# Four weight blocks of the first unit: GpSimd makes the last two high parts of each

## The reference, cut to what matters

```
u    = rms_norm(x, norm_gain)
proj = jnp.einsum('btd,dc->btc', u, w_in).astype(f32)
```

## Time and profile before

| | |
|---|---|
| median of 3 runs | 2012.45 us |
| profiled execution | 2012.38 us |
| its span, first to last instruction | 2010.6 us |
| TensorE busy | 1960.3 us (98%), 12974 matmuls |
| VectorE busy | 1667.5 us (83%) |
| ScalarE busy | 876.1 us (44%) |
| GpSimd busy | 309.4 us (15%), 288 instructions |
| mean granted TensorE clock | 0.99 |

### The profile page before, as it was taken

The page is one execution under the profiler, slowest core; times in us unless marked ns, Lnnn a source line. Parts: engine busy times, 40 slices in busy tenths (PEclk is TensorE's granted clock), DMA queues, the critical chain, the costliest instruction groups (busy, mean ns, idle before and its releaser), DMA issues.

```text
span 2010.6 us, 36659 instructions
## 1 busy us (share of the span) xinstructions
PE 1960.3 (98%) x12974; PEld 1095.1 (54%) x12974; DVE 1667.5 (83%) x4034; ACT 876.1 (44%) x2246; POOL 309.4 (15%) x288
## 2 busy tenths in 40 slices
PE   6999999999999999999999999999999999999998
PEld 4555555555555555444465555555555555554453
DVE  7888888888888888664478888888888888898757
ACT  7844444444444446231265444444444444452100
POOL 3011111111111112120011111111111111111100
PEclk9999999999999999999999999999999999999989
DMA  9222222222222224885542232222222222458552
GB/s 338 54 41 61 51 50 50 50 62 58 50 50 50 50 62 133 192 264 155 177 142 61 57 65 50 50 50 50 54 59 54 60 50 50 107 142 198 140 136 95
DMA packets 303428, 184.17 MB, mean 92 GB/s; under 512 B 267847, under 2 KB 277000, under 8 KB 303180
## 3 DMA queue, kind: packets, MB, share of 16 engines
q1 hardware_dynamic: 287348, 151.41, 30.5%
q0 software_dynamic: 7424, 29.43, 4.1%
q10 hardware_dynamic: 8568, 2.18, 0.5%
HBM read 85.29 MB, written 41.06 MB: 63 GB/s over the span
## 4 chain that ended last, share of the span: by engine, by line
PE 85%; DVE 10%; ACT 2%; issue 2%; DMA 1%; SPq 0%; DVEq 0%; ACTq 0%
PE J L593 53%; PE J L1338 13%; PE W L1031 2%; PE W L1020 2%; PE W L1107 2%; PE W L1137 1%; PE J L1071 1%; PE W L1125 1%; PE W L1096 1%; PE T L1116 1%; ACT W L577 1%; DMA ST<-ST 1%; PE W L1038 1%; PE T L1081 1%; PE W L1109 1%
## 5 line engine op out<-in xcount | busy, mean ns | idle before, releaser
L593 PE MATMUL J<-W,uT_mix 128*128 128x512 f16 (+2 forms) x3072 | 609.1, 355 | 5.1 <-DVE W L584 4.3
L593 PE MATMUL J<-W,x_mix 128*128 128x512 f16 (+2 forms) x3072 | 604.4, 353 | 3.6 <-issue 2.2
L593 PEld LDWEIGHTS J<-W,uT_mix 128*128 128x128 f16 x3072 | 296.8, 99 | 275.6 <-issue 11.3
L593 PEld LDWEIGHTS J<-W,x_mix 128*128 128x128 f16 x3072 | 295.6, 98 | 270.9 <-issue 7.0
L1454 ACT ACTIVATE PB<-J,out_scale 128x512 f32<-128x512 f32 (+2 forms) x224 | 133.1, 594 | 286.6 <-PE J L593 278.4
L1338 PE MATMUL J<-W,EM_qkR_mix 128*128 128x512 f16 x480 | 115.3, 379 | 0.0
L2414 POOL TENSOR_TENSOR ST<-HH,ge 128x512 f32<-128x512 f32 x32 | 41.4, 1294 | 408.9 <-DVE HH L1884 408.9
L2423 POOL TENSOR_TENSOR ST<-ST,ge 128x512 f32<-128x512 f32 x32 | 67.9, 2121 | 216.0 <-DVE ST L1929 216.0
L1418 ACT ACTIVATE sc_xr<-sc_xr,small 128x128 f32<-128x128 f32 x256 | 98.5, 386 | 0.0
L1338 PE MATMUL J<-W,x_mix 128*128 128x512 f16 x400 | 98.0, 384 | 0.0
L1424 ACT ACTIVATE ST<-ST,small 128x1024 f16<-128x1024 f32 x32 | 36.7, 1148 | 140.2 <-DVE small L1945 140.2
(11 more groups left out here) (470 smaller groups left out, 3479.1 us busy)
## 6 DMA issues: line engine op xcount, KB each, us to landing
W<-in_w_in POOLq DMA_DIRECT2D x8, 2048.0 KB, 11.1
mix_d<-ST SPq DMA_DIRECT2D x32, 512.0 KB, 2.6
sc_xr<-in_x_prompt SPq DMA_DIRECT2D x20, 512.0 KB, 4.1
sc_xr<-x SPq DMA_DIRECT2D x20, 512.0 KB, 3.8
ST<-in_w_in POOLq DMA_DIRECT2D x4, 2048.0 KB, 11.9
W<-in_w_out SPq DMA_DIRECT2D x4, 2048.0 KB, 7.9
PB<-in_x_prompt SPq DMA_DIRECT2D x6, 512.0 KB, 3.8
x<-PB SPq DMA_DIRECT2D x6, 512.0 KB, 3.5
```

The costliest lines, as they stand in the source:

```text
L593: mm = nc.tensor.matmul(out, stationary(k, a), moving[:, k, b, :], start=(k == 0 and n == 0), stop=(k == KT - 1 and n == 2))
```

## The change

In layer 0 only, for blocks j = 4 to 7, ScalarE makes slices 0 to 5 of the high part (`HI_ACT = 6`), and a new function, `block_hi_end`, makes slices 6 and 7 on GpSimd with `tensor_scalar`. Each of GpSimd's slices waits for the block's scale, for the low part of the same slice of the block before, and for the count of `C["hi"]` up to it, so that the count stays in order. ScalarE's `block_hi` of blocks 5 to 7 gets a wait for all the high parts of the block before. On GpSimd the eight new multiplications stand after `first_rope` and the last load, ahead of `r_gate`.

```diff
+        HI_ACT = 6
 ...
         def block_hi(act, layer, j, ks=range(KT)):
 ...
+            if layer == 0 and j > 4:
+                act.wait_ge(C["hi"], KT * j)
 ...
+        def block_hi_end(pool, layer, j):
+            b = SAMPLE_ORDER[j]
+            pool.wait_ge(C["scale_ready"], NBLK * layer + j + 1)
+            for k in range(HI_ACT, KT):
+                pool.wait_ge(C["lo"], KT * (NBLK * layer + j - 1) + k + 1)
+                pool.wait_ge(C["hi"], KT * (NBLK * layer + j) + k)
+                nc.gpsimd.tensor_scalar(pair[b][:, k, 0, :], raw(layer, b)[:, k, :], gs[:, j, k:k + 1], None, ALU.mult
+                                        ).then_inc(C["hi"], 1)
 ...
-                block_hi(act, layer, 4)
+                block_hi(act, layer, 4, range(0, HI_ACT))
 ...
-                block_hi(act, layer, 5)
+                block_hi(act, layer, 5, range(0, HI_ACT))
 ...
-                block_hi(act, layer, 6, range(5, KT))
+                block_hi(act, layer, 6, range(5, HI_ACT))
 ...
-                block_hi(act, layer, 7)
+                block_hi(act, layer, 7, range(0, HI_ACT))
 ...
                 load_raw(pool, layer, "mvo")
+            else:
+                for j in range(4, NBLK):
+                    block_hi_end(pool, layer, j)
             c_pool.begin(pool, N0)
             r_gate(N0)
             m_gate(N0)
```

## The result

Five runs of the changed kernel took 2022.91 to 2029.55 us, median 2026.21; the kernel before, run beside it, 2008.77 to 2014.11. The ratio is 1.0064, 95% interval 1.0049 to 1.0079: slower by 12.9 us (9.9 to 15.9). The direction was forecast; 5.8 us and a range up to 2021.5 were not enough. The profiled execution took 2022.91, span 2021.1, mean granted clock 0.988.

What follows compares the result with a forecast made beforehand. TensorE was taken as the bound, with 85% of the chain. Block 4 at 0, blocks 5 to 7 at 3 x 2.04, less 0.4 and 0.25, plus 0.3, gave 5.8 us: 2012.38 to 2018.2, range 2013.5 to 2021.5.

Steps and rivals of the forecast that it cites:

- What is removed: Eight ScalarE multiplications, 5.0 us of ScalarE's time, none on the chain, so priced at 0.
- In series with VectorE: Blocks 5 to 7: GpSimd's multiplications and VectorE's low parts exclude each other, delaying each block's last low part 2.04 us.
- Rival 1: GpSimd gets its turn between two low parts without holding VectorE up; time 2012.0, not slower; chance 0.17.
- The forecast of 0 for block 4: Block 4: TensorE's slack of 2.7 us and VectorE's 2.50 idle hide the 2.04 us delay, costing 0.
- The price p: Time of one GpSimd multiplication of the new kind, taken as 0.85 us, with ends 0.61 and 1.27.
- d: Delay of a block's last low part, 2p + 0.34, where p is one GpSimd multiplication: 2.04 us, 1.56 to 2.88.
- The smaller terms: Block 7: 0.4 won at L2072 beside `r_gate`, 0.25 of TensorE's slack, 0.3 lost to `r_gate`.
- Rival 2: The clock falls as well, TensorE pausing twice in each of three products; one fall 2.9 us, 2021.1; chance 0.09.
- My row against it: Evidence against a clock fall: from 68 to 70 us TensorE was busy 0.88 of 2.00, the clock stayed at 1.00.
- Rival 3: First `tensor_scalar` on GpSimd pays for set-up, block 4's last low part passing its slack by 2 us; 2020.2; chance 0.04.

Runs made afterwards that it cites:

- the zero fill: Changed kernel with GpSimd only filling slices 6 and 7 of the high part with zero, reading nothing; ratio 1.0002 against the kernel before.
- the load alone: Kernel before, ScalarE making all slices, plus GpSimd repeating the eight multiplications into scratch that nobody reads; ratio 1.0007.
- the run of block 5 alone: Changed kernel with GpSimd making slices 6 and 7 of block 5 only; ratio 1.0026 against the kernel before.
- the run with one slice: Changed kernel with HI_ACT 7 instead of 6, so GpSimd makes slice 7 alone in blocks 4 to 7; ratio 1.0028 against the kernel before.
- two tensors: Changed kernel with GpSimd's multiplication as a two-tensor one, the scale column repeated 512 times; one run, 2023.21 us.
- with gaps: Changed kernel with a short VectorE reduction ahead of the low parts of slices 3, 4 and 5 of blocks 5 to 7; one run, 2021.12 us.
- second set: The changed kernel timed and profiled once more with no edit; ratio 1.0058 against the kernel before.
- its own count: Changed kernel with GpSimd's slices counting on their own semaphore, not waiting for ScalarE's slices 0 to 5; ratio 1.0015 against the kernel before.
- the run with both repairs: Changed kernel with GpSimd's slices on their own semaphore, not waiting for ScalarE's, and made as two-tensor multiplications; ratio 1.0004 against the kernel before.

## Why the prediction was wrong, step by step

- **What is removed: right.** ScalarE's 5.0 us were priced at 0; the zero fill, with the same relief, gives 29.8 and 1.0002.
- **In series with VectorE: right in blocks 5 to 7, wrong in block 4.** In blocks 5 to 7 VectorE idles before slices 6 and 7 with GpSimd as the releaser, slice 6 is the long one in block 5 (4.17 for 2.05), and the load alone costs 0.7. In blocks 6 and 7 it is hardly longer than slice 7 (2.18 and 2.19 for 2.05), since ScalarE's slice 5 came late. Rival 1 is out there. In block 4 it is what happened: GpSimd had its turns between low parts, and the last one came 0.7 us late, not 2.04. The forecast of 0 for block 4 held, but not for its reason.
- **The price p: the step that failed.** I took 0.85, from rows of another operation, and let it end at 1.27, the row of two full tensors. It measured 1.55 alone, and 1.44 from the end of VectorE's low parts. The formula was sound: 2 x 1.44 + 0.34 = 3.2 for d, measured 3.1 in block 5 and in the run of block 5 alone. With it the prediction's sum is 3 x 3.22 - 0.35 = 9.3 us, or 2021.7, just past the range's end; the clock makes the rest. What I had worked out from the row with the small operand, 1.03, is what the two-tensor form takes (1.02); I carried it to another instruction. The rule that "GPSIMD Engine Reference", section 4.1, of the Trainium skill states, one input at roughly line rate, gave 0.62; the measurement is 2.5 times that, and decides.
- **The smaller terms: right.** L2085 beside nothing takes 0.34 where it took 0.82, 0.48 won for 0.4 said; the last low part of block 7 takes 1.20 for 0.75, so `r_gate` cost 0.45 for 0.3 said.
- **Rival 2, the clock, came on top.** I gave it 0.09. Both profiles of the changed kernel have falls, in block 5 and in or behind block 7. In the first the price is 0.64 + 0.2 in block 5 (last slice, spread) and 0.64 + 0.9 in block 7 (last slice; the score products behind it end 1.9 us after it where they took 1.04 before), 2.4 in all. My row against it was one pause of 1.1 us; the change makes two in a product, 2.1 to 2.8 us together, with 0.8 us of work between them. One such pause (the run with one slice) or two of 0.9 (two tensors) brought no fall, and the pair in block 5 alone none in its profile. Nor did the pairs of block 6, in the changed kernel and with gaps (1.32 and 1.39). So a fall is not certain, its cause stays open, and the row with one pause did not speak for the pair.
- **The sum with both:** 3 x 3.1 - 0.48 - 0.25 + 0.45 = 9.0, plus 2.4 of clock is 11.4; the stretch grew by 11.3. The timed 12.9 and 11.7 us (second set, 1.0058) agree within their intervals. With p in the range I had, as with two tensors, the same path gives 5.3 in its profile.
- **Rival 3: out.** The first `tensor_scalar` took 1.78 us, with no gap ahead of it beyond the wait for ScalarE.

## What to carry to other kernels

A freed engine was worth nothing here, where it was already ahead; ask first which engine the low parts, the products and the scales wait for. The price of an operation that has no row in the trace went by its form here, not by its size and number of inputs: measure it alone before it is put between two steps of the path. If GpSimd must help beside VectorE's two-tensor operations, let it start before they do (its own count here took the stretch's 11.3 us down to 0.6), and read the granted clock behind every pause of TensorE.

## What the runs showed of the hardware

- On GpSimd, `tensor_scalar` from float32 to float16 with a scalar per row, 128x512, takes 1.55 us alone; the two-tensor multiplication with that scalar repeated takes 1.02. A fill of that size takes 0.58, and ran beside unbroken low parts.
- `tensor_scalar` shuts VectorE out for a part of its length only. In block 4 its second one (57.68 to 59.26) got in between low parts; the low part behind it took 1.17 for 0.74, so it was held up 0.43 us, not 1.44. A two-tensor multiplication beside low parts held VectorE up for 0.9 (blocks 6 and 7 of the run with both repairs).
- Whether GpSimd gets in between back-to-back low parts differs: it did in block 4 of the changed kernel, in both profiles, and not in blocks 5 to 7. In block 4 its first one began at 55.73, just before a short reduction of VectorE (L541, 55.99 to 56.26). In the run with one slice GpSimd began behind that reduction, at 56.73, and was kept out until the low parts ended (4.67 us). But the second one in block 4 of the changed kernel got in with no reduction near. The runs don't show why.
